# Forty-two runs of unread TensorE products behind the end of a three-block model kernel

## The chip, the cores and the metric

The kernel runs as one program on one core of a Trainium2 chip. The metric is the device time in microseconds from start to end of the program, as the median of its timed executions. Engines are named as in the profile: PE is the matrix engine (PEld its weight loads), ACT the scalar engine, DVE the vector engine, POOL and SP the other two, of which SP issues most of the DMAs.

## What is computed

The reference is a chain of transformer blocks over 256 tokens of width 1024 in float32: two layers that mix attention and a long convolution for a token stream and a context stream, then one layer of dilated attention with cross attention to a memory, and at its end a mixture of 32 experts. Only the last step, the final norm of the one output (1 x 256 x 1024), is near the change:

```python
y = tf * lax.rsqrt(jnp.mean(tf * tf, axis=-1, keepdims=True) + NORM_EPS)
return (y * g.astype(jnp.float32)).astype(t.dtype)
```

## The kernel before

Each engine has a program of its own, written out in order (`tensor_program`, `scalar_program`, `vector_program`, `pool_program`, `sync_program`); they wait for each other through counting semaphores. A name such as `pe_sums.up("spread", "output")` raises a semaphore when an instruction ends, and `at(...)` with the same name is what another engine waits for. `banks` deals out the eight PSUM banks of 128 partitions by 512 float32 columns in turn; `banks.emptied(...)` is the wait for the former user of a bank.

Activations lie with features on the partitions and tokens in the columns. A weight is cut into tiles of 128 by 128. Most dense layers run in a split form (`SPLIT`, `pe_block` at line 446, `pe_pair`): weights and activations are each split into a rounded part and a remainder, both of type float32r, and a product of a tile is three single pass products, (rounded, rounded), (rounded, remainder), (remainder, rounded), accumulated over eight tiles of the feature dimension. That makes 24 PE products for an output block, each with its own weight load of 128 columns. In the first layer the moving operand has 512 columns (256 tokens and 256 of the context), in the later layers 256. The rounding is ACT's (line 434, `ACT.Copy` from float32 to float32r, 1024 columns at a time), the remainder DVE's (line 442). A product in plain float32 is two PE instructions in the trace.

The line of PE that fills waits is `pe_idle` (line 546): float32 products of the constant tile `ones` with itself, into a bank that nobody reads, so that PE isn't idle ahead of a dense stretch:

```python
for i in range(n):
    ins = pe.eng.matmul(out[:, 0:P], ones[:, :], ones[:, :], start=True, stop=True)
```

`area` is a buffer of 14336 columns a partition, with a view `area_r` of type float32r at the same addresses; through most of the kernel it holds activations, and in the mixture of experts weights of experts.

The end of the program is one chain. The last expert's output is scattered back and added (PE line 2531, DVE line 2539), ACT squares it (line 556), PE sums the squares over the features with `ones` (line 2717), ACT takes the root (line 568), DVE the reciprocal (line 579), PE spreads it over the partitions (`pe_spread`, line 539, signal `("spread", "output")`), DVE scales by it (line 591), and SP sends the result out in four DMAs (line 2735) and waits for them. PE has nothing to do after `pe_spread`, ACT nothing after line 568.

Of the kernel before, what the change touches and what calls it, by code (L numbers as in the profile page):

```python
# [13 lines left out]
ACT = mybir.ActivationFunctionType  # L14
AX = mybir.AxisListType

P = 128
# [4 lines left out]
UF, EF = UB * P, EB * P  # L22
# [248 lines left out]
def two_blocks_kernel(nc, T):  # L271
    ctx = ExitStack()
    with ctx:
# [3 lines left out]
        def sb2(name, cols):  # L277
            at = (nc.sbuf_base + 31) // 32 * 32
            t = sb(name, cols)
            return t, nc.alloc_sbuf_tensor_at(name + "_r", [P, cols], F32R, offset=at)  # L280
# [6 lines left out]
        area, area_r = sb2("area", 14336)  # L287
# [103 lines left out]
        banks = Slots([b[:, :] for b in psum])  # L391
# [8 lines left out]
        def vv(key, i=0, n=1, rows=P):  # L400
            return vec[0:rows, VEC[key] + i:VEC[key] + i + n]
# [89 lines left out]
        def pe_open(pe, site, read_by=None, root_read_by=None):  # L491
            banks.hold(read_by or (ve_norm, ("used", site)), "sum", site)
            rsts.take(root_read_by or (pe_sums, ("spread", site)), site)
# [13 lines left out]
        def pe_added(site):  # L507
            for n in range(7):
                squares.take((ve_squares, ("added", site, max(n, 1))), site, n)
            squares.take((pe_sums, (site, 7)), site, 7)  # L510
# [24 lines left out]
        def pe_spread(pe, site, cols, give=True):  # L535
            pe.wait_ge(*landed["con"])
            pe.wait_ge(*ve_norm.at("rstd", site))
            for tb in range(cols // P):
                ins = pe.eng.matmul(banks.ap("sum", site)[:, tb * P:(tb + 1) * P],
                                    rsts.ap(site)[:, tb:tb + 1].to_broadcast([P, P]), ident, start=True, stop=True)  # L540
            ins.then_inc(*pe_sums.up("spread", site))
            if give:
                banks.give("sum", site)


        def pe_idle(pe, site, n):
            out = banks.take((pe_sums, ("idle", site)), "idle", site)
            pe.wait_ge(*banks.emptied("idle", site))
            pe.wait_ge(*gp_start.at("ones"))
            for i in range(n):  # L550
                ins = pe.eng.matmul(out[:, 0:P], ones[:, :], ones[:, :], start=True, stop=True)
            ins.then_inc(*pe_sums.up("idle", site))

        def ac_square(ac, site, n, chunk, cols):
            ac.wait_ge(*squares.emptied(site, n))
            ac.eng.activation(squares.ap(site, n)[:, 0:cols], chunk, ACT.Square).then_inc(*ac_squares.up(site, n))
# [2151 lines left out]
        def pe_output(pe):  # L2708
            pe_open(pe, "output")
            out = banks.ap("sum", "output")  # L2710
            pe.wait_ge(*banks.emptied("sum", "output"))
            for pair in range(4):
                s = squares.take((pe_sums, ("output", pair)), "output", pair)
                pe.wait_ge(*ac_squares.at("output", pair))
                for c in range(2):
                    for tb in range(2):
                        ins = pe.eng.matmul(out[:, tb:tb + 1], s[:, 256 * c + tb * P:256 * c + (tb + 1) * P], ones[:, 0:1],
                                            start=pair + c + tb == 0, stop=pair == 3 and c + tb == 2)
                ins.then_inc(*pe_sums.up("output", pair))
            pe_spread(pe, "output", N)  # L2720

        def ac_output(ac):
            for pair in range(4):
                ac.wait_ge(*ve_experts.at("added", 7, pair))
                ac_square(ac, "output", pair, X2[:, 2 * pair:2 * pair + 2, :], 512)
            ac_sqrt(ac, "output", 4, N, 1024)
# [9 lines left out]
            sp.wait_ge(s_out, 64)  # L2736


        def tensor_program(pe):
            pe_mod_group(pe, 0)  # L2740
            pe_mod_group(pe, 1)
            pe_open(pe, "mix0")
            pe_added("mix0")
            pe.wait_ge(*gp_start.at("ones"))
            pe_sum_seven(pe, "mix0", 512)
            pe_sum_last(pe, "mix0", 512)
            pe_spread(pe, "mix0", 512)
            pe_mod_group(pe, 2)
            pe_mod_group(pe, 3)
            pe_idle(pe, "mix0", 12)  # L2750
            for l in range(2):
                pe_heads(pe, l)
                pe_hyena(pe, l)
                for n, a in enumerate(attention(l)):
                    pe_attend(pe, a, convolving(l, n, pe_conv_step))
                pe_merge(pe, l)
                pe_mix_out(pe, l)
                pe_gate_up(pe, l)
                pe_down(pe, l)
            pe_keys(pe)  # L2760
            pe_mixer(pe)
            pe_mixed(pe)
            pe_memory(pe)
            pe_router_steps(pe)
            pe_moe(pe)
            pe_output(pe)

        def scalar_program(ac):
            ac.eng.dma_start(vec[:, :], T["vecs"]).then_inc(*landed["vec"])
            ac.eng.dma_start(con[:, 0:NCON0], T["con"][:, 0:NCON0]).then_inc(*landed["con"])  # L2770
            ac.wait_ge(*landed["vec"])
            for s, name in enumerate(("c", "c_ctx")):
                ac.eng.activation(tc1[:, 8 * s:8 * s + 8], vv(name, 0, 8), ACT.Sigmoid).then_inc(*ac_mod.up("silu", s))
            ac_mod_group(ac, 0)
            ac.wait_ge(*landed["x"])
            for k in range(8):
                ac_square(ac, "mix0", k, X[:, k, :], 512)
            ac_mod_group(ac, 1)
            ac_sqrt_table(ac, 5, 8)
            ac_sqrt(ac, "mix0", 8, 512, 1024)  # L2780
            ac_mod_group(ac, 2)
            ac_split(ac, where["w_in", 0, 1])
            ac_mod_group(ac, 3)
            ac_norm_mod(ac, "mix0", 0, 512)
            for l in range(2):
                if l:
                    ac_norm_mod(ac, "mix1", 1, 512)
                ac_heads(ac, l)
                ac_hyena(ac, l)
                ac.eng.activation(st[:, 41:42], epsc[:, 0:1], ACT.Exp)  # L2790
                for n, a in enumerate(attention(l)):
                    ac_attend(ac, a, convolving(l, n, ac_conv_step))
                ac_merge(ac, l)
                ac_mix_out(ac, l)
                ac_norm_mod(ac, f"ffn{l}", l, tokens(l))
                ac_gate_up(ac, l)
                ac_down(ac, l)
            ac_keys(ac)
            ac_mixer(ac)
            ac_mixed(ac)  # L2800
            ac_memory(ac)
            ac_router_steps(ac)
            ac_moe(ac)
            ac_output(ac)

        def vector_program(ve):
            ve.eng.memset(sc2[:, :, :], 0.0).then_inc(*ve_mod.up("zero"))
# [234 lines left out]
```

## Time and profile before

| | |
|---|---|
| time, median of 2 runs | 2091.78 us (2089.67 and 2093.88) |
| the profiled execution | 2084.13 us |
| its span (first to last instruction or transfer) | 2082.3 us |
| mean granted clock of PE in it | 0.967 of full speed |
| PE busy | 1890.6 us, 91% of the span |
| PE weight loads busy | 1553.5 us, 75% |
| DVE busy | 1145.1 us, 55% |
| ACT busy | 903.1 us, 43% |

The profiled execution's time is 1.8 us over its span, and 7.65 us under the median of the timed runs. Busy times are of one execution. A product's duration in the trace reaches from its start to its modelled end, and products overlap: how fast a stretch of them goes is read from the distance of their starts, or from the length of a stretch and its count.

### The profile page before, as it was taken

What the parts mean: (1) busy time and instruction counts of PE and PEld (TensorE: products, weight loads), DVE (VectorE), ACT (ScalarE), POOL (GpSimd) and SP (SyncE); (2) the same over time, 40 slices, a digit from 0 to 9 for tenths busy, and PEclk for the clock granted to TensorE, in tenths of its full rate; (3) what the DMA queues carried; (4) which work ended last, traced back from release to release, by engine and by line L of the source; (5) the groups of instructions that cost most, each with busy time, mean ns of one, the idle gap of its engine ahead of it and who ended that gap; (6) DMA issues with size and microseconds to landing.
All of it is one profiled execution on the core that took longest, in us unless ns stands there. A gap on an engine that the chain in (4) does not pass through costs nothing.

```text
span 2082.3 us, 33838 instructions
## 1 busy us (share of the span) xinstructions
PE 1890.6 (91%) x14190; PEld 1553.5 (75%) x14190; DVE 1145.1 (55%) x1878; ACT 903.1 (43%) x1532; POOL 16.9 (1%) x31
## 2 busy tenths in 40 slices
PE   7999989999999999999999999999999777667666
PEld 4877668888778888798699999997898544455343
DVE  3454766776887788557666667789665111110012
ACT  4333445665756667455454555634845000000001
POOL 0000000000000000000000000000000000000000
PEclk9999999999999999999999999999999988888898
DMA  8222014553555555224056555543247999999996
GB/s 321 83 71 81 1 71 154 180 182 111 180 175 180 192 190 174 91 91 153 1 182 203 172 183 189 178 162 112 83 151 316 420 420 420 419 418 420 420 420 249
DMA packets 91121, 428.00 MB, mean 206 GB/s; under 512 B 11089, under 2 KB 12754, under 8 KB 66002
## 3 DMA queue, kind: packets, MB, share of 16 engines
q1 hardware_dynamic: 78866, 382.51, 49.4%
q10 hardware_dynamic: 12096, 43.26, 6.2%
q8 instruction: 114, 1.87, 0.4%
q14 instruction: 45, 0.37, 0.1%
HBM read 424.68 MB, written 1.05 MB: 204 GB/s over the span
## 4 chain that ended last, share of the span: by engine, by line
PE 68%; DMA 19%; DVE 5%; ACT 4%; issue 2%; SPq 1%; ACTq 0%; POOL 0%; DVEq 0%; POOLq 0%
PE bank L463 41%; PE bank L1619 8%; DMA area<-in_w 8%; DMA ring<-in_w 4%; DMA his<-in_w 4%; DMA PPT<-in_w 3%; PE bank L1198 2%; PE bank L478 2%; PE bank L2508 2%; PE bank L2464 1%; PE bank L1171 1%; PE bank L1100 1%; PE bank L2115 1%; PE bank L937 1%; PE bank L1186 1%
## 5 line engine op out<-in xcount | busy, mean ns | idle before, releaser
L442 DVE TENSOR_TENSOR ring_r<-ring,his_r 128x1024 fp32r<-128x1024 f32 x314 | 383.2, 1222 | 223.8 <-ACT his_r L434 222.3
L463 PE MATMUL bank<-HH_r,his_r 128*128 128x256 f32 (+1 forms) x1504 | 498.3, 331 | 1.6 <-DVE ring_r L442 1.6
L463 PE MATMUL bank<-HH_r,ring_r 128*128 128x256 f32 (+1 forms) x1504 | 490.8, 326 | 0.0
L463 PE MATMUL bank<-H_r,his_r 128*128 128x256 f32 (+1 forms) x1440 | 471.6, 328 | 0.0
L434 ACT ACTIVATE his_r<-ring 128x1024 fp32r<-128x1024 f32 x314 | 330.7, 1056 | 302.8 <-PE bank L463 272.1
L463 PEld LDWEIGHTS bank<-HH_r,his_r 128*128 128x128 f32 x1504 | 283.5, 188 | 35.2 <-issue 8.6
L463 PEld LDWEIGHTS bank<-HH_r,ring_r 128*128 128x128 f32 x1504 | 283.4, 188 | 24.7
L463 PEld LDWEIGHTS bank<-H_r,his_r 128*128 128x128 f32 x1440 | 270.7, 188 | 27.2 <-issue 1.0
L2480 DVE TENSOR_TENSOR tmp<-tmp,bank 128x128 f32<-128x128 f32 x64 | 18.4, 287 | 384.3 <-ACT tmp L2473 257.2
L463 PE MATMUL bank<-area_r,his_r 128*128 128x256 f32 (+1 forms) x480 | 148.9, 323 | 0.0
L2464 PE MATMUL bank<-area,KF 128*32 128x128 f32 x1888 | 89.2, 312 | 47.5 <-DMA area<-in_w 38.9
L1619 PE MATMUL bank<-VT_r,ring_r 128*128 128x512 f32 (+1 forms) x352 | 118.6, 337 | 0.0
L2464 PEld LDWEIGHTS bank<-area,KF 128*32 128x32 f32 x1888 | 71.5, 126 | 62.8 <-DMA area<-in_w 49.5
L1619 PE MATMUL bank<-YF_r,his_r 128*128 128x512 f32 (+1 forms) x352 | 118.3, 336 | 0.0
L1619 PE MATMUL bank<-VT_r,his_r 128*128 128x512 f32 (+1 forms) x352 | 117.6, 334 | 0.0
L463 PEld LDWEIGHTS bank<-area_r,his_r 128*128 128x128 f32 x480 | 89.8, 189 | 7.6
L2519 ACT ACTIVATE H<-bank 128x512 f32<-128x512 f32 x16 | 9.6, 597 | 187.7 <-PE bank L2508 187.7
L712 ACT ACTIVATE rst<-rst 128x1024 f32<-128x1024 f32 x80 | 83.5, 1044 | 0.6 <-DVE rst L704 0.6
L2508 PE MATMUL bank<-area,tmp 128*32 128x512 f32 x256 | 55.5, 643 | 22.3 <-DMA area<-in_w 22.3
L1346 ACT ACTIVATE VT_r<-area 128x512 fp32r<-128x512 f32 (+1 forms) x96 | 49.9, 523 | 51.0 <-PE bank L1619 45.3
L1619 PEld LDWEIGHTS bank<-YF_r,his_r 128*128 128x128 f32 x352 | 66.1, 188 | 7.7
L1619 PEld LDWEIGHTS bank<-VT_r,his_r 128*128 128x128 f32 x352 | 66.2, 188 | 7.5 <-DVE YF_r L1350 0.2
(418 smaller groups left out, 3316.9 us busy)
## 6 DMA issues: line engine op xcount, KB each, us to landing
area<-in_w SPq DMA_DIRECT2D x91, 1024.0 KB, 27.3
ring<-in_w_in SPq DMA_DIRECT2D x102, 512.0 KB, 3.5
ring<-in_w_gate_up SPq DMA_DIRECT2D x88, 512.0 KB, 3.5
ring<-in_w SPq DMA_DIRECT2D x36, 1024.0 KB, 27.0
HH<-in_w SPq DMA_DIRECT2D x26, 1024.0 KB, 26.8
ring<-in_w_down SPq DMA_DIRECT2D x44, 512.0 KB, 4.3
KX<-in_w_mod_rows ACTq DMA_DIRECT2D x28, 512.0 KB, 3.4
VX<-in_w_mod_rows ACTq DMA_DIRECT2D x28, 512.0 KB, 3.5
```

The costliest lines, as they stand in the source:

```text
L434: ac.eng.activation(hi_slot(n), stream.slot(u), ACT.Copy).then_inc(*ac_hi.up(n))
L442: ve.eng.tensor_tensor(lo_slot(u), stream.slot(u), hi_slot(n).bitcast(F32), ALU.subtract).then_inc(*ve_lo.up(n))
L463: ins = pe.eng.matmul(out, a, b, start=k == 0 and m == 0, stop=end)
L478: ins = pe.eng.matmul(out, a, b, start=k + m == 0, stop=k == 7 and m == 2)
L712: ac.eng.activation(prod, prod, ACT.Copy, accum_out=MODS[l][:, j, s:s + 1]).then_inc(*ac_mod.up("sum", n, s))
L937: ins = pe.eng.matmul(vb[tb // 2][:, o:o + 256], x[:, k, sl], w, start=k == 0 and n == 0 and o == 0, stop=k == 7 and n == 2 and o > 0)
L1100: ins = pe.eng.matmul(b, cc(nm, 256 * tb + fb * P), VT[:, 2 * s + tb, :], start=tb == 0, stop=tb == 1)
L1198: ins = pe.eng.matmul(out[:, 0:256], vs(kc), c.pts[g % 2][:, kc * 256:(kc + 1) * 256], start=kc == 0, stop=kc == c.nk - 1)
L1346: ac.eng.activation(hi, src, ACT.Copy).then_inc(*ac_cut.up(*key))
L1619: ins = pe.eng.matmul(banks.ap("ff", l, 4 * half + n)[:, 0:t], w, x, start=k == 0 and i == 0, stop=k == 21 and i == 2)
L2464: ins = pe.eng.matmul(out[32 * n:32 * n + 32, 0:P], HG[g % 2][:, k, 32 * j:32 * j + 32], w, start=k == 0, stop=k == 7, tile_position=(0, 3 ...
L2508: ins = pe.eng.matmul(out[32 * j:32 * j + 32, :], AT[j][:, 32 * k:32 * k + 32], w, start=k == 0, stop=k == 3, tile_position=(0, 32 * j))
```

## The change

`tensor_program` gets `pe_bench` as its last step, and `scalar_program` a last step of 14 copies. Nothing that was there is touched: no instruction is removed or moved.

- ACT, once PE has spread the final norm, rounds the whole of `area` in place to float32r, in 14 instructions of 1024 columns. The last one signals `bench`.
- PE waits for that signal, and issues `pe_idle` with 40 products.
- Then come 21 runs with 512 columns of moving operand and 21 with 256. A run is one accumulation into a bank: 24 single pass products for 512 columns (8 tiles, 3 passes), 48 for 256 columns (twice 8 tiles, 3 passes). Behind each run stands one product of 64 columns into the same bank, with the signal of the run. That is 504 products of 512 columns, 1008 of 256 and 42 of 64.
- The first run of each width is the plain one (tiles and passes as in the kernel's split form, weights at column 0 and 1024 of `area_r`, moving operands at 4096 and 8192). The others differ from it in one thing: weights begin 8, 16, 32 or 64 columns later; moving operands 8, 16 or 32 columns later; the second moving operand lies 16 or 256 columns beyond 4096 from the first; the same weights each time, the same moving operand each time, or both; another order of the passes; all weights from column 12288 or 2048; one column repeated as the moving operand (step 0); one column repeated as the weights; weights with a step of two columns; a moving operand with a step of two columns. The last, 21st run is the plain one again, its products dealt in turn to two banks.
- No one reads the banks, and `area` is not used again.

```diff
--- before.py
+++ after.py
@@ -2736,6 +2736,41 @@
             sp.wait_ge(s_out, 64)
 
 
+        def bench_plain(n, w0=0, m0=0, low=4096, same_w=False, same_m=False, order=((0, 0), (0, 1), (1, 0)), w_at=0, m_at=4096):
+            out = []
+            for k in (list(range(8)) if n > 256 else list(range(8)) * 2):
+                for wl, ml in order:
+                    w = w_at + (0 if same_w else 1024 * wl + P * k) + w0
+                    m = m_at + (0 if same_m else low * ml + 512 * k) + m0
+                    out.append((area_r[:, w:w + P], area_r[:, m:m + n]))
+            return out
+
+        def bench_runs(n):
+            wide = [(w, area_r[:, 4096:4097].to_broadcast([P, n])) for w, _ in bench_plain(n)]
+            flat = [(area_r[:, 0:1].to_broadcast([P, P]), m) for _, m in bench_plain(n)]
+            apart = [(area_r[:, 0:2 * P:2], m) for _, m in bench_plain(n)]
+            spread = [(w, area_r[:, 4096:4096 + 2 * n:2]) for w, _ in bench_plain(n)]
+            return [bench_plain(n), bench_plain(n, w0=8), bench_plain(n, w0=16), bench_plain(n, w0=32), bench_plain(n, w0=64),
+                    bench_plain(n, m0=8), bench_plain(n, m0=16), bench_plain(n, m0=32), bench_plain(n, low=4096 + 16),
+                    bench_plain(n, low=4096 + 256), bench_plain(n, same_w=True), bench_plain(n, same_m=True),
+                    bench_plain(n, same_w=True, same_m=True), bench_plain(n, order=((0, 0), (1, 0), (0, 1))),
+                    bench_plain(n, w_at=12288), bench_plain(n, w_at=2048), wide, flat, apart, spread]
+
+        def pe_bench(pe):
+            pe.wait_ge(*ac_out.at("bench"))
+            pe_idle(pe, "bench", 40)
+            for n in (512, 256):
+                for r, run in enumerate(bench_runs(n) + [bench_runs(n)[0]]):
+                    two = [banks.take((pe_sums, ("bench", n, r)), "bench", n, r, i) for i in range(2)]
+                    for i in range(2):
+                        pe.wait_ge(*banks.emptied("bench", n, r, i))
+                    last = int(r == len(bench_runs(n)))
+                    for i, (w, m) in enumerate(run):
+                        out = two[i % 2 * last]
+                        pe.eng.matmul(out[:, 0:n], w, m, start=i <= last, stop=i >= len(run) - 1 - last)
+                    pe.eng.matmul(two[0][:, 0:64], area_r[:, 0:P], area_r[:, 0:64], start=True, stop=True).then_inc(
+                        *pe_sums.up("bench", n, r))
+
         def tensor_program(pe):
             pe_mod_group(pe, 0)
             pe_mod_group(pe, 1)
@@ -2764,6 +2799,7 @@
             pe_router_steps(pe)
             pe_moe(pe)
             pe_output(pe)
+            pe_bench(pe)
 
         def scalar_program(ac):
             ac.eng.dma_start(vec[:, :], T["vecs"]).then_inc(*landed["vec"])
@@ -2802,6 +2838,10 @@
             ac_router_steps(ac)
             ac_moe(ac)
             ac_output(ac)
+            ac.wait_ge(*pe_sums.at("spread", "output"))
+            for i in range(14):
+                ins = ac.eng.activation(area_r[:, i * UF:(i + 1) * UF], area[:, i * UF:(i + 1) * UF], ACT.Copy)
+            ins.then_inc(*ac_out.up("bench"))
 
         def vector_program(ve):
             ve.eng.memset(sc2[:, :, :], 0.0).then_inc(*ve_mod.up("zero"))
```

## Rows read from the trace of the kernel before

**Rows 1.** The page: the span, and the busy time of PE and ACT.

```profile
span 2082.3 us, 33838 instructions
PE 1890.6 (91%) x14190; PEld 1553.5 (75%) x14190; DVE 1145.1 (55%) x1878; ACT 903.1 (43%) x1532; POOL 16.9 (1%) x31
```

**Rows 2.** The chain that ended last, its end: start us, us, what.

```profile
2071.45 3.52 PE bank L2717 x32
...
2075.51 0.72 PE bank L539 x4
2076.24 0.02 issue
2076.26 0.48 DVE H L591
2076.74 0.39 DVEq L273
2077.13 2.35 DVE H L591 x6
```

**Rows 3.** Timeline of all engines from 2076: start us, us, engine and line.

```profile
2076.26 3.22 DVE L591 SCALAR_TENSOR_TENSOR H<-X,vec,bank 128x256 f32<-128x256 f32 x8 [0.80 <-PE bank L539]
2077.16 2.72 SPq L2735 DMA_DIRECT2D out<-H  x4
```

**Rows 4.** Windows at the end: PE, PEld, DVE, ACT, POOL busy, granted clock, DMA.

```profile
2070.00:2076.00 6.00, 5.45 (x43) 5.21 (x41) 1.99 (x4) 2.40 (x5) 0.00 (x0) 1.00 0.00 0
2076.00:2082.00 6.00, 0.22 (x2) 0.03 (x1) 3.22 (x8) 0.00 (x0) 0.00 (x0) 0.54 0.53 175
```

**Rows 5.** Timeline of ACT, three roundings in a row at 304.

```profile
304.60 2.93 ACT L434 ACTIVATE his_r<-ring 128x1024 fp32r<-128x1024 f32 x3
```

**Rows 6.** Groups by line and form, ACT's roundings: count, busy us, mean ns.

```profile
L434 ACT ACTIVATE his_r<-ring 128x1024 fp32r<-128x1024 f32 x314 | 330.7, 1056 | 302.8 <-PE bank L463 272.1 <-PE bank L2115 8.3 <-PE bank L937 8.2
```

**Rows 7.** Timelines of PE, two stretches of `pe_idle` with 14 products.

```profile
499.01 3.29 PE L551 MATMUL bank<-ones 128*128 128x128 f32 x28
...
885.45 4.83 PE L551 MATMUL bank<-ones 128*128 128x128 f32 x28
```

**Rows 8.** Windows over the second of these and after it, columns as above.

```profile
885.40:888.70 3.30, 3.30 (x18) 3.30 (x17) 2.23 (x4) 2.22 (x5) 0.69 (x2) 0.50 0.02 5
888.70:890.00 1.30, 1.30 (x13) 1.30 (x13) 1.30 (x3) 1.27 (x3) 0.82 (x1) 1.00 0.00 0
```

**Rows 9.** The chain, dense stretches with 512 columns.

```profile
161.93 38.49 PE bank L463 x168
...
307.58 187.20 PE bank L463 x816
...
626.42 131.84 PE bank L463 x576
```

**Rows 10.** The chain, dense stretches with 256 columns.

```profile
947.38 32.66 PE bank L463 x288
...
1153.32 65.29 PE bank L463 x576
...
1231.25 39.58 PE bank L463 x336
...
1270.83 56.80 PE bank L1619 x480
```

**Rows 11.** Windows over dense stretches of both widths, columns as above.

```profile
162.00:200.00 38.00, 38.00 (x167) 31.21 (x166) 19.08 (x22) 11.87 (x14) 0.00 (x0) 1.00 0.26 83
626.00:758.00 132.00, 132.00 (x577) 108.27 (x577) 100.13 (x98) 85.12 (x137) 0.00 (x0) 1.00 0.57 185
```

**Rows 12.** Timeline of PE where one-column products interrupt a dense stretch.

```profile
1218.32 0.28 PE L463 MATMUL bank<-HH_r,ring_r 128*128 128x256 f32 x1
1218.44 0.50 PE L516 MATMUL bank<-ones,tmp 128*128 128x1 f32 x4
1218.81 0.59 PE L523 MATMUL bank<-ones,tmp 128*128 128x1 f32 x4
1219.25 0.36 PE L463 MATMUL bank<-HH_r,his_r 128*128 128x256 f32 x1
1219.45 0.28 PE L463 MATMUL bank<-H_r,his_r 128*128 128x256 f32 x1
```

**Rows 13.** Groups by line and form, products of 512 columns from various tiles.

```profile
L463 PE MATMUL bank<-HH_r,ring_r 128*128 128x512 f32 x624 | 245.2, 393 | 0.0
...
L1619 PE MATMUL bank<-YF_r,his_r 128*128 128x512 f32 x176 | 69.0, 392 | 0.0
...
L463 PE MATMUL bank<-area_r,his_r 128*128 128x512 f32 x176 | 66.4, 392 | 0.0
```

## What it will do to the time

> **What bounds the kernel now.** I began with the page [rows 1]: PE is busy for 91% of 2082.3 us, so the body of the kernel is PE's. But the diff touches none of the body, so what counts is what the end of the span hangs on. The chain of waits, read at its end [rows 2], shows it: PE's last product, the spread of the norm (L539), ends at 2076.23, DVE scales for the remaining time, and the four output DMAs start beside it [rows 3]. The window from 2076 to 2082 shows PE and ACT with nothing to do, and a granted clock of 0.54 in the mean, so mostly the lower level of 1.2 GHz [rows 4]. The reader should see two things: between the spread and the end lie only 6.1 us, and this is all the cover that new work on ACT and PE can have. Everything in the change waits for that spread, so nothing of it can slide forward under the dense body.
>
> **The work ahead of the runs.** ACT waits for the spread. DVE began 0.02 us after it [rows 2]; ACT should begin as early, at 2076.26. It then makes 14 roundings of 1024 columns, the same instruction as L434, which takes 1056 ns by itself [rows 6]. In a row they overlap a little: three take 2.93 us [rows 5], so (2.93 - 1.06) / 2 = 0.94 us from start to start. 13 x 0.94 + 1.06 = 13.3 us, to 2089.6. That the source and target are the same columns changes nothing that the rows would show; ACT touches nothing else. The waits of this kernel's engines on each other cost 0.02 to 0.05 us, so PE starts at 2089.65.
>
> PE then issues 40 idle products, which are 80 instructions, as 14 are 28 in the trace. At the full clock 28 take 3.29 us from the first start to the last end [rows 7]; taking off the last one's 0.28 leaves 27 distances of 0.1115 us. 80 of these are 8.9 us. PE has then been idle for 13 us and sits at the lower level. The second stretch of 28 shows the price: 4.83 us instead of 3.29, and its first 3.3 us stand at a granted clock of 0.50, after which it is 1.00 [rows 7, 8]. So one such stretch at the low level costs 1.5 us; two would cost some 3.1. I take a value between, 2.4, and so 11.3 us. PE stands at 2100.9, at 2.4 GHz, when the runs begin.
>
> **The runs.** The plain runs repeat the order of the kernel's own split products, so the dense stretches are the rows to use. With 512 columns: 168 in 38.49, 816 in 187.20, 576 in 131.84 us [rows 9], which is 229.1, 229.4 and 228.9 ns each. I take 229.0: 504 x 0.229 = 115.4 us. With 256 columns there are two paces: 288 in 32.66 and 576 in 65.29 are 113.4 ns, 336 in 39.58 and 480 in 56.80 are 117.8 and 118.3 [rows 10]. The pace holds through a whole stretch and changes only after an interruption, such as the one-column products at 1218 [rows 12]: 113 ahead of them, 117.8 behind. The bench interrupts itself after every run with a product of 64 columns, and more of the long stretches stand at the slower pace, so I take 117.8: 1008 x 0.1178 = 118.7 us. All at the faster pace would be 114.3, which is 4.4 less.
>
> Is that pace right for a bench that runs alone, with no DMA and an idle DVE and ACT? A stretch with a DMA share of 0.26 and ACT busy for a third of it goes at 229.1, one with 0.57 and ACT busy for two thirds at 228.9 [rows 9, 11]. So I see no contention that could fall away. The Trainium skill, page "TensorE: Matmul & The Clock Gate", section Back-to-back issue gap, gives N / 2.4 + 2.5 ns for a single product's gap, that is 215.8 and 109.2 ns here. By that rule the runs would take 108.8 + 110.1 = 218.9 us rather than 234.1, and the total would come out 15.2 lower; the trace disagrees with it for float32r at both widths, by 13 ns at 512 columns.
>
> **Between the runs.** The 42 products of 64 columns are cheaper than a weight load: a product of one column, two instructions each, keeps a distance of about 0.1 us (eight instructions from 1218.44 to 1219.25, 0.81 us) [rows 12]. The next product's successor then came 0.20 instead of 0.118 us later [rows 12], a further 0.08. So a boundary costs 0.10 to 0.19 us; I take 0.15, and 42 x 0.15 = 6.3 us. The waits for the banks cost nothing: the bank of a run was last used by a run about three before it, or by work finished ahead of the spread, except the spread's own bank, which DVE has done with by 2079.5 [rows 3], 10 us ahead.
>
> **The odd operands.** Offsets of 8 to 64 columns, repeated tiles, other passes, other places in `area`: the rows show products from `HH_r`, `YF_r` and `area_r` with weights from two buffers, all at 392 or 393 ns of duration [rows 13], so I cost these at nothing. A gain is excluded only at 512 columns by the 213.3 ns that the columns themselves need at 2.4 GHz. No row has a moving operand or weights with a step of two or zero. From below: a step costs nothing. From above, each fetch takes twice as long: for the moving operand 24 x 0.213 + 48 x 0.107 = 10.2 us for both widths; for the weights, with 0.1115 us as the distance that a weight load allows [rows 7], 0.223 is still hidden under 0.229 at 512 columns, and at 256 costs 48 x (0.223 - 0.118) = 5.0. Together 15.2 us. I take the lower end, since the rows closest to them, all with a step of one, show the pace set by neither the tile nor its place.
>
> The Trainium skill, page "SBUF — State Buffer", section Door 1, says that two hits in a line of 16 bytes suffice for full bandwidth. By that rule a step of two float32 columns costs nothing; no run here shows it yet.
>
> **The sum.** 2076.26 + 13.3 + 0.05 + 11.3 + 115.4 + 118.7 + 6.3 = 2341.3, and 0.3 for the last product's end: a span of 2341.6 against 2082.3, 259.3 us more. With the 1.8 us around the span the profiled execution would go from 2084.1 to 2343.4. The median of the timed runs stands 7.65 us above it; I add to the median: 2091.8 + 259.3 = 2351.1 us. The output DMAs, at the end before, end 250 us early and drop off the chain.
>
> **The rivals.** First, the forecast with steps that cost (chance 0.20): one or both of the stepped fetches, or an offset or a place in `area`, halves the rate of a run. One width of a doubled run costs about 5 us, all four cases together 15.2: 2356 to 2366. For it: these are the things that no row covers. Against it: two of the forty-two runs each way are all that can be hit so.
>
> Second, the columns alone set the pace (0.06). If what adds 16 ns to each product of 512 columns is the other engines' work, it goes away behind the end: 512 / 2.4 GHz is 213.3 ns, 256 is 106.7, together 107.5 + 107.5 = 215.0 instead of 234.1, and 2332 us. Against it stands the comparison of stretches with little and much beside them [rows 9, 11]. The rule of the Trainium skill's TensorE page, told above, would put the time at 2336, close to this.
>
> Third, the clock stays low (0.03). If something in these runs, such as repeated operands, keeps PE at 1.2 GHz throughout, columns take 426.7 and 213.3 ns: 215.0 + 215.0 = 430 us, 196 more, 2547 us. Against it: the level rose within one stretch of idle products [rows 8], and it is 1.00 through every dense stretch [rows 11].
>
> Fourth, the other side: not slower (0.03). The products are read by nobody. If the build drops work without a reader, neither ACT's copies nor the runs exist, the price falls to nothing and the time is 2091.8. It would decide as soon as unread results are removed at all. Against it: the idle products have no reader either, and they stand in the trace, 28 and 28 of them [rows 7]. Hiding can't give this result, for the cover is 6.1 us and the work 265.
>
> **How the numbers follow.** The forecast as summed has 0.68. Its own range: 4.4 down for the fast pace, 2 either way for the boundaries, 1 for the idle products, and the 7.65 us between median and profiled execution, since it isn't known where the next median falls: 2340 to 2356. Reaching into the first rival gives 2338 to 2366, which holds about 0.8. A measurement of this kernel can tell a change of about 2% from none, 42 us; the forecast is 12.4% slower, and only the fourth rival is inside. Slower 0.97, same 0.03, faster 0.
>
> **What would show it.** In the profile after: the body unchanged up to 2076; a block of 14 ACT instructions of 13.3 us, PE idle under it; 80 instructions of L551 in about 11 us, of which the first 3 to 7 at 0.5 of the clock; then a PE timeline with 504 starts 0.229 apart and 1008 starts 0.113 or 0.118 apart, the granted clock at 1.00 to the end, and DMA at zero. The runs with a step of two and those with one repeated column are the last ones of each width ahead of the plain repeat, so a cost of theirs shows as longer spacing there alone. The forecast is wrong if the spacing of the plain run differs from the kernel's own, if a boundary shows a gap of half a microsecond, or if any odd run is slowed by more than a fifth.

## The result, and the profile after

The changed kernel takes 2361.87 us (median of 2 runs, 2359.17 and 2364.57) against 2091.78: a ratio of 1.129, with a 95% interval of 1.127 to 1.132. The forecast was 2351, with a range of 2338 to 2366.

The page of the kernel after, its first lines and the sum of the new products:

```profile
span 2357.4 us, 37123 instructions
PE 2154.4 (91%) x15824; PEld 1791.1 (76%) x15824; DVE 1145.8 (49%) x1878; ACT 916.8 (39%) x1546; POOL 16.9 (1%) x31
...
L2770 PE MATMUL bank<-area_r 128*128 128x256 f32 (+1 forms) x1512 | 250.4, 328 | 0.0
```

It answers to [rows 1]. PE gained 1634 instructions: 80 idle ones, 1512 products and 42 of 64 columns. ACT gained 14, DVE none.

The chain that ended last, in order of time, around the end of the old kernel and through the runs of 512 columns (L2843 are the roundings, L551 the idle products, L2770 the runs, L2771 the products of 64 columns):

```profile
2081.65 0.72 PE bank L539 x4
2082.38 0.02 issue
2082.40 2.95 ACT area_r L2843 x3
2085.35 0.95 ACTq L273
2086.30 9.47 ACT area_r L2843 x10
2095.77 0.04 issue
2095.81 11.10 PE bank L551 x80
2106.91 5.47 PE bank L2770 x24
2112.38 0.03 PE bank L2771
2112.41 5.67 PE bank L2770 x24
...
2163.36 5.55 PE bank L2770 x24
...
2196.84 5.33 PE bank L2770 x24
...
2202.20 5.64 PE bank L2770 x24
...
2207.87 5.73 PE bank L2770 x24
...
2213.63 10.93 PE bank L2770 x24
...
2224.60 5.55 PE bank L2770 x24
```

and at the end, with 256 columns:

```profile
2317.16 5.83 PE bank L2770 x48
...
2323.02 5.45 PE bank L2770 x48
...
2328.51 5.68 PE bank L2770 x48
...
2334.22 5.85 PE bank L2770 x48
...
2340.10 11.10 PE bank L2770 x48
...
2351.24 5.83 PE bank L2770 x48
```

Read it against the order of the variants. A plain run takes 5.55 us, one with the weights 8 columns later 5.67 (2112.41). The last five of each width are: one column repeated as moving operand (5.33 and 5.45), one column repeated as weights (5.64, 5.68), weights with a step of two (5.73, 5.85), the moving operand with a step of two (10.93 and 11.10), and the plain run again. So one variant of twenty is dear, and it costs 10.7 us over both widths: 10.93 - 5.55 and 11.10 - 5.83.

The end of the span moved by 275.1 us. The spread of the norm ends at 2082.37, where it ended at 2076.23 [rows 2]: 6.1 us are in the body, which the change doesn't touch. From the spread to the end it is 275.03 us instead of 6.07, so the new work is worth 269.0 us.

The 6.1 us of the body are in part a lottery that the rows of before already hinted at. The same 576 products of a dense stretch with 256 columns, in the chain after:

```profile
1158.19 68.08 PE bank L463 x576
```

They took 65.29 us in the profile before [rows 10]: 118.2 ns a product against 113.4, in the same code. Of the twelve profiles taken of kernels with this body, the changed kernel and the experiments without padding among them, two show this stretch settled at 113.3 ns and ten at 117.8, and none shows anything between. The most of the 6.1 us arose earlier: the stretch that starts at 626.42 in the profile of before [rows 9] starts at 631.04 here, and no run was made to find out why. Seven runs of the kernel before, taken beside the first experiment, spread over 2089.26 to 2101.5 us, so a body longer by 6 us is nothing unusual.

### The profile page after: what moved, and what is told of

Its sections match the earlier page's. It is cut to its first block, busy times and chain, and to the rows that moved or that the text cites. A ratio compares the mean times of both kernels' runs of the same rounds, so it can differ in the third digit from the quotient of the medians.

```text
span 2357.4 us, 37123 instructions
## 1 busy us (share of the span) xinstructions
PE 2154.4 (91%) x15824; PEld 1791.1 (76%) x15824; DVE 1145.8 (49%) x1878; ACT 916.8 (39%) x1546; POOL 16.9 (1%) x31
## 3 DMA queue, kind: packets, MB, share of 16 engines
HBM read 424.68 MB, written 1.05 MB: 181 GB/s over the span
## 4 chain that ended last, share of the span: by engine, by line
PE 68%; DMA 17%; DVE 7%; ACT 4%; issue 2%; SPq 1%; ACTq 0%; POOL 0%; POOLq 0%; DVEq 0%
PE bank L463 36%; PE bank L2770 11%; PE bank L1619 7%; DMA area<-in_w 6%; DMA ring<-in_w 4%; DMA his<-in_w 2%; DMA PPT<-in_w 2%; PE bank L2464 1%; PE bank L478 1%; PE bank L1198 1%; DMA con<-in_w 1%; DMA HH<-in_w 1%; DVE st L1270 1%; PE bank L2115 1%; PE bank L2508 1%
## 5 line engine op out<-in xcount | busy, mean ns | idle before, releaser
L463 PEld LDWEIGHTS bank<-HH_r,his_r 128*128 128x128 f32 x1504 | 282.8, 188 | 36.8 <-issue 11.6
L2770 PE MATMUL bank<-area_r 128*128 128x256 f32 (+1 forms) x1512 | 250.4, 328 | 0.0
L2770 PEld LDWEIGHTS bank<-area_r 128*128 128x128 f32 x1512 | 218.5, 191 | 25.6 <-issue 5.6
L1619 PE MATMUL bank<-VT_r,his_r 128*128 128x512 f32 (+1 forms) x352 | 118.6, 337 | 0.0
L1619 PE MATMUL bank<-YF_r,his_r 128*128 128x512 f32 (+1 forms) x352 | 117.5, 334 | 0.0
L1619 PEld LDWEIGHTS bank<-VT_r,ring_r 128*128 128x128 f32 x352 | 66.0, 187 | 7.7
```

The source lines that it names most:

```text
L463: ins = pe.eng.matmul(out, a, b, start=k == 0 and m == 0, stop=end)
L1619: ins = pe.eng.matmul(banks.ap("ff", l, 4 * half + n)[:, 0:t], w, x, start=k == 0 and i == 0, stop=k == 21 and i == 2)
L2770: pe.eng.matmul(out[:, 0:n], w, m, start=i <= last, stop=i >= len(run) - 1 - last)
```

## The experiments

In the experiments the "settled" spacing of a run is the mean of the last twelve distances between the starts of its products in the trace; its first few distances are longer while it settles.

**The stepped operand alone.** The edit:

```diff
-            spread = [(w, area_r[:, 4096:4096 + 2 * n:2]) for w, _ in bench_plain(n)]
+            spread = bench_plain(n)
```

> The moving operand with a step of two columns is replaced by the plain operands, in one run of each width. My theory (the step doubles the time of a product, the one odd operand that costs in full): these two runs fall from 11.0 and 11.1 us to 5.6 and 5.8 us, all others stay, so 10.6 to 10.7 us go, and the ratio to the kernel before falls from 1.129 to 1.124. Rival (the two runs are slow for their place in the order, or for what ran before them): they stay above 10 us and the ratio stays.

Measured: 2350.65 us (median of 4), a ratio of 1.122 with an interval of 1.118 to 1.125, which holds 1.124 and no longer holds 1.129. The run in the place of the dear one, in the chain, with its neighbours:

```profile
2211.36 5.73 PE bank L2770 x24
...
2217.12 5.54 PE bank L2770 x24
...
2222.70 5.55 PE bank L2770 x24
```

With 256 columns the run in that place took 5.86 us instead of 11.14, from its start to the next run's. From the end of the spread to the start of the last run it is 257.8 us instead of 268.7, 10.9 less. The step was the cause, and the place was not.

**What a step costs.** The twenty variants are exchanged for steps and pieces; the core of the edit:

```diff
+            def mv(step):
+                return [(w, area_r[:, 4096:4096 + step * n:step]) for w, _ in bench_plain(n)]
+            def wt(step):
+                return [(area_r[:, 0:step * P:step], m) for _, m in bench_plain(n)]
+            def part(a, b):
+                return [(w, area_r[:, 4096:4096 + n // a * b].rearrange("p (x y) -> p x y", y=b)[:, :, 0:a]) for w, _ in bench_plain(n)]
```

> The 20 variants of each width are exchanged: moving operands with a step of 1, 2, 3, 4, 8 and 0 columns; moving operands in pieces, 2 of 4 columns, 4 of 8, 8 of 16, 2 of 3, 16 of 32; weights with a step of 1, 2, 3, 4, 8 and 0; both with a step of two. Theory A (any gap between neighbouring columns breaks a paired read of two columns, so each column is read alone): every step above 1 gives 452 and 228 ns a product, and pieces of two or more adjacent columns stay near 230 and 118. Theory B (the bytes spanned count): step 3 gives about 680 ns, step 4 about 900, 2 of 4 columns as slow as a step of two, about 452. Theory C (two hits in a line of 16 bytes suffice, as the notes say): a step of 2 and 2 of 4 are alike, and a step of 4 is slower than a step of 2. Weights: in the changed kernel a step of two cost only 3% at 512 columns and nothing at 256, where a halved rate of loading would show as about 228 ns; if loading has no paired read, steps of 3, 4 and 8 cost no more either.

Settled spacings, worked out from the starts in the trace, in ns:

| moving operand | 512 columns | 256 | weights | 512 | 256 |
|---|---|---|---|---|---|
| contiguous | 226.7 | 120.0 | contiguous | 226.7 | 120.0 |
| step 2 | 453.3 | 230.0 | step 2 | 233.3 | 120.0 |
| step 3 | 450.0 | 226.7 | step 3 | 235.5 | 173.3 |
| step 4 | 461.5 | 233.3 | step 4 | 236.7 | 233.3 |
| step 8 | 431.1 | 217.8 | step 8 | 244.4 | 240.0 |
| step 0 | 218.6 | 112.0 | step 0 | 231.7 | 113.3 |
| 2 of 4 | 453.3 | 230.0 | | | |
| 2 of 3 | 340.0 | 173.3 | | | |
| 4 of 8 | 233.3 | 117.8 | both operands with step 2 | 453.3 | 233.3 |
| 8 of 16 | 233.3 | 120.8 | | | |
| 16 of 32 | 240.0 | 120.0 | | | |

Theory A fails at 2 of 4: adjacent columns, and still twice the time. Theory B fails at steps of 3, 4 and 8, which cost no more than 2. Theory C fails too: a step of two columns of float32, two hits in 16 bytes, costs the moving operand all of a doubling. For the weights it costs 7 ns at 512 columns and nothing at 256. Larger steps cost the weights 9 to 18 ns at 512 columns and 53 to 120 at 256; that the long products hide most of a slower load is my reading, and no run separates it.

**Pieces.** Sixteen shapes of pieces and steps, cut as above with a first column of choice.

> The 20 variants of each width are moving operands in pieces: 2 of 4 columns beginning at column 0, 1 and 3 of a group of four; 2 of 8; 4 of 8 beginning at 0, 1 and 2; 4 of 5; 4 of 6; 4 of 12; 8 of 12 beginning at 0 and 2; 16 of 20 beginning at 0 and 2; steps of 5, 6 and 16; plain ones beginning 1 or 2 columns later. Theory D, formed on the steps run: the moving operand is read in aligned groups of four columns; a group of which two or more are wanted takes the time of four columns, one with a single wanted column the time of two. That gives, as multiples of the time of a contiguous operand (227 to 233 ns at 512 columns): 2 for all of 2 of 4 and 2 of 8; 1 for 4 of 8 at 0 and 4 of 12; 1.5 for 4 of 8 at 1, 2 for it at 2; 1.25 for 4 of 5; 1.5 for 4 of 6; 1 and 1.5 for 8 of 12; 1 and 1.25 for 16 of 20; 2 for the steps; 1 for a shift by 1 or 2. Rival E (a gap costs by the piece, whatever its place): 4 of 8 costs the same at 0, 1 and 2, and 8 of 12 and 16 of 20 at 0 and 2.

At 512 columns, in multiples of the contiguous 226.7 ns: 2 of 4 from column 0, 1 and 3 and 2 of 8: 2.0; 4 of 8 from 0: 1.02, from 1: 2.0, from 2: 2.0; 4 of 5: 1.25; 4 of 6: 1.5; 4 of 12: 1.0; 8 of 12 from 0: 1.03, from 2: 1.5; 16 of 20 from 0: 1.06, from 2: 1.25; steps of 5, 6 and 16: 1.9 to 2.0; shifted by 1 or 2 columns: 1.05 and 1.02. Rows of the chain, 4 of 8 from column 0, 1 and 2:

```profile
2155.98 5.63 PE bank L2775 x24
2161.64 10.94 PE bank L2775 x24
2172.61 10.99 PE bank L2775 x24
```

Rival E is out: the place within a group of four columns (16 bytes) decides. Theory D is right but for 4 of 8 from column 1, where it wanted 1.5.

**A rule for groups, tried on new shapes.**

> Seventeen new shapes of moving operand and three of weights, to try a rule fitted to the two runs before. Theory G: PE fetches the moving operand in accesses of four cycles; one access brings those next wanted columns that lie in one aligned group of four, and at least the next two wherever they lie. Theory D (as in the pieces run): a group with two or more wanted columns costs four cycles, with one wanted column two. Theory T: every touched group costs four. Times over a contiguous operand (227 to 233 ns at 512 columns), G / D / T: 4 of 8 from column 3: 2 / 1.5 / 2; 4 of 7: 1.75 / 1.5 / 1.75; 4 of 9: 1.5 / 1.5 / 1.75; 2 of 5: 2 / 2 / 2.5; 2 of 6 from column 3: 2 / 2 / 3; 2 of 7: 2 / 2 / 2.5; 8 of 9: 1.125 by all; 8 of 10: 1.25 by all; 8 of 12 from 1 or from 3 and 8 of 16 from 1: 1.5 / 1.25 / 1.5; 4 of 10: 1.5 by all; 8 of 11: 1.375 / 1.25 / 1.375; 16 of 17: 1.06 by all; 2 of 5 from 3: 2 / 2 / 2.5; 4 of 6 from 2: 1.5 by all. Weights with a step of 5, 6 and 16 at 256 columns: 233 to 240 ns like steps of 4 and 8, if each touched group costs a weight load four cycles.

There were sixteen shapes of the moving operand, not seventeen. Measured (settled, at 512 columns, over 226.7): 4 of 8 from 3: 2.09; 4 of 7: 1.56; 4 of 9: 1.50; 2 of 5: 2.01; 2 of 6 from 3: 2.00; 2 of 7: 2.03; 8 of 9: 1.15; 8 of 10: 1.25; 8 of 12 from 1 and from 3: 1.50; 8 of 16 from 1: 1.44; 4 of 10: 1.54; 8 of 11: 1.28; 16 of 17: 1.07; 2 of 5 from 3: 2.03; 4 of 6 from 2: 1.53. Weights with steps of 5, 6 and 16 at 256 columns: 228.1, 228.9 and 220.0. Theory G is near in fourteen of sixteen and wrong at 4 of 7 and 8 of 11, where D is right; D is wrong at the four shapes of 4 or 8 columns that begin at 1 or 3; T is wrong at every shape of pairs that it put above 2, and at 4 of 7, 4 of 9 and 8 of 11. The weights came out 4 to 20 ns under the 233 to 240 expected. What stands: full aligned groups of four go within 6% of full pace, a cut group mostly costs as if it were whole (less at 4 of 7, 4 of 9 and 8 of 11), and nothing costs much more than twice (2.09 at most). The exact rule for cut groups stays open.

**Where the operands begin.** Plain runs whose weights begin w and moving operands m columns later:

```diff
+            pairs = ((0, 0), (8, 0), (16, 0), (24, 0), (32, 0), (40, 0), (48, 0), (56, 0), (4, 0), (0, 4), (0, 8), (0, 16), (0, 32),
+                     (0, 48), (8, 8), (16, 16), (32, 32), (16, 32), (48, 48), (32, 16))
+            return [bench_plain(n, w0=a, m0=b) for a, b in pairs]
```

> The 20 variants of each width are exchanged for plain runs whose weights begin w columns later and whose moving operands m columns later, with w and m from 0 to 56. In the changed kernel the settled spacing at 512 columns was 226 to 227 ns for the plain run and for offsets of 64 or 256, and 231 to 237 in the mean for 8, 16 and 32. Theory A (the distance of the two operands modulo 64 columns counts): (8,8), (16,16), (32,32) and (48,48) are back at 226 to 227, and (16,32) is like (0,16). Theory B (each operand's own start counts): (16,16) is slow like (16,0) or (0,16). At 256 columns the plain run had 120 to 121.5, and an offset of 16 in either operand 113 to 115; theory A then gives 121.5 for (16,16), theory B 113 to 115.

Settled spacings by the distance w - m, modulo 64 columns:

| distance | runs (w, m) | 512 columns | 256 columns |
|---|---|---|---|
| 0 | (0,0) (8,8) (16,16) (32,32) (48,48) | 226.7 in all | 120.0 in all |
| 4 | (4,0) | 226.7 | 118.7 |
| 8 | (8,0) | 233.3 | 118.6 |
| 16 | (16,0) (0,48) (32,16) | 233.3 in all | 113.3 in all |
| 24 | (24,0) | 234.6 | 117.5 |
| 32 | (32,0) (0,32) | 232.5, 232.9 | 118.2, 120.0 |
| 40 | (40,0) | 233.3 | 120.0 |
| 48 | (48,0) (0,16) (16,32) | 228.9 in all | 117.8 in all |
| 56 | (56,0) (0,8) | 233.3 in both | 116.7 in both |
| 60 | (0,4) | 231.7 | 113.3 |

Theory A holds, theory B falls at (16,16) and each other equal pair. What counts is how far apart the two reads begin, modulo 64 columns or 256 bytes, and not where either begins. With 256 columns the distance doesn't settle it alone: the run (0,16) has 117.8 ns here and had 113.3 in the changed kernel.

**Carried over to the body.** Adding up the allocations, each rounded up to 8 columns, puts the body's weights 48 columns from its activations. The edit, in the kernel before and without a bench, with 16 and with 32 columns:

```diff
+        pad = sb("pad", 16)
         ring, ringr = sb2("ring", NS * UF)
```

> The kernel before, without any bench, with an unused buffer of 16 columns ahead of the weight ring, so that ring and rounded weights begin 16 columns later and the activations stay. Theory A carried over to the body (the distance of weights and moving operand modulo 64 columns sets the pace): adding up the allocations puts the body's weights 48 columns from the moving operands, and 48 is the distance whose bench runs settle at 228.9 and at 117.8 or 113.3, as the body does. With the pad the distance is 0: the dense stretches of 512 columns go from 229.0 to 226.7 ns, those of 256 from 117.8 or 113.3 to 120.0. Rival (the body's 229.0 has other causes, such as the waits for weights or other engines): 229.0 and 117.8 stay.

> As the run before, with 32 columns: a distance of 16, whose bench runs settle at 233.3 ns at 512 columns and at 113.3 or 117.8 at 256. Theory A: dense stretches of 512 columns at 233.3, of 256 at 113.3 or 117.8. Rival: 229.0 and 117.8 stay.

The chain of the kernel with 16 columns of padding, the stretches that answer to two of [rows 9, 10]:

```profile
627.58 130.59 PE bank L464 x576
...
1157.78 69.24 PE bank L464 x576
```

and with 32 columns:

```profile
634.60 134.40 PE bank L464 x576
...
1163.46 68.08 PE bank L464 x576
...
1244.18 38.09 PE bank L464 x336
```

576 products of 512 columns took 131.84 us before; they take 130.59 (226.7 ns each) at distance 0 and 134.40 (233.3) at distance 16. With 256 columns all dense stretches of the first pad settle at 119.4 to 120.4 ns, and those of the second at about 113.3 or 117.8, in turns. An unused buffer of 64 bytes a partition moves the pace of the body's dense stretches, just as the bench says. It makes no better kernel that anything here shows: what one width gains the other loses, and the single runs, 2098.42 and 2092.95 us beside 2090.82, lie within the spread of the kernel before. A layout with distance 0 for the wide layers and 16 for the rest was not tried.

**Is it the company?** ACT and DVE work beside the runs, until some 2320 of 2363.6 us, in buffers that no run reads:

```diff
+            for i in range(230):
+                if i >= 3:
+                    ac.wait_ge(*ac_angles.at("busy", i - 3))
+                ac.eng.activation(his_flat[:, i % 3 * UF:(i % 3 + 1) * UF], hh_flat[:, 0:UF], ACT.Copy).then_inc(*ac_angles.up("busy", i))
+            for i in range(200):
+                if i >= 6:
+                    ve.wait_ge(*ve_angles.at("busy", i - 6))
+                ve.eng.tensor_tensor(ring[:, i % 6 * UF:(i % 6 + 1) * UF], hh_flat[:, UF:2 * UF], hh_flat[:, 2 * UF:3 * UF], ALU.subtract).then_inc(*ve_angles.up("busy", i))
```

> ACT makes 230 copies and DVE 200 subtractions of 1024 columns beside the runs, in buffers that no run reads, so the bench no longer runs alone. My theory (other engines' work on SBUF doesn't reach PE's reads; the kernel's own 229 ns and 117.8 ns come from where its operands lie): the runs keep their spacing within 0.5 ns, 5.58 us a plain run of 512 columns, 5.86 of 256. Rival (the second rival of the prediction turned round: what other engines do costs PE some ns a product): the plain runs of 512 columns rise from a settled 226.7 to 229 ns or more, 24 x 2.3 ns = 0.06 us or more a run, and the whole bench by 1 to 3 us.

The windows over the runs of 512 columns, first of the changed kernel, then of this one (columns as in [rows 4]):

```profile
2107.00:2230.00 123.00, 123.00 (x525) 97.45 (x524) 0.00 (x0) 0.00 (x0) 0.00 (x0) 1.00 0.00 1
```

```profile
2113.00:2237.00 124.00, 124.00 (x532) 98.41 (x531) 124.00 (x110) 124.00 (x132) 0.00 (x0) 1.00 0.00 1
```

DVE and ACT went from nothing to fully busy. From the first run's start to the last run's start it is 244.43 us against 244.41. The work of the other two engines costs PE nothing here. This run has no DMAs beside it, but the padded body has: at distance 0 its 512 column products come 226.7 ns apart with DMAs, ACT and DVE at work, like the plain run of the bench that is alone.

**The product of 64 columns.** Left out, the run's last product signals:

```diff
-                    pe.eng.matmul(two[0][:, 0:64], area_r[:, 0:P], area_r[:, 0:64], start=True, stop=True).then_inc(
-                        *pe_sums.up("bench", n, r))
+                    ins.then_inc(*pe_sums.up("bench", n, r))
```

> The 42 products of 64 columns are gone; the last product of a run signals. In the changed kernel the start of a 64 column product is followed by the next run's first product after 29 to 31 ns, and that by the second after 313 (512 columns) or 200 (256) instead of some 231 and 118. My theory (the 64 columns are too few to hide the weight load behind them, so its rest lies open once a run): without them a boundary looks like any other pair of products, the first distance of a run is about 231 and 118, and 42 x 0.11 = 4.7 us go from the bench. Rival (the opening of an accumulation in another bank or the signal costs): the first distance stays near 313 and 200, and only 42 x 0.03 = 1.2 us go.

The chain now shows one piece:

```profile
2111.09 245.85 PE bank L2770 x1512
```

The changed kernel needed 250.2 us for the same products and the 42 narrow ones (2106.91 to 2357.10): 4.3 us, 0.10 a run. The first distance of a run of 512 columns is 226 to 237 ns instead of some 313, apart from the very first run (314) and the runs of and right behind the repeated and the stepped operand, whatever bank it opens. So the cost was the narrow product's, as expected, and not that of the bank or the signal; why it costs this, my theory of the open weight load, isn't shown. The runs at distance 16 and 48 with 256 columns settled at 117.8 ns here and at 113.3 in the changed kernel.

**One run, twenty phases.** All variants are the plain run with the moving operands 16 columns later, and ahead of run r stand r products of 96 columns:

```diff
+            return [bench_plain(n, m0=16) for _ in range(20)]
...
+                    for _ in range(r):
+                        pe.eng.matmul(two[0][:, 0:96], area_r[:, 0:P], area_r[:, 0:96], start=True, stop=True)
```

> All 20 variants of a width are the same run, the moving operands 16 columns later, which at 256 columns settled at 113.3 in the changed kernel and at 117.8 in the offsets run, just as the dense stretches of the body settle at 113.3 or 117.8. Ahead of run r stand r products of 96 columns, so that the run starts at another phase. My theory (two patterns of product and weight load that each sustain themselves, chosen at the start of a stretch): within this kernel some runs of 256 columns settle at 113.3 and others at 117.8, and none between; at 512 columns all settle at 228.9. Rival (the pace is a matter of what lies where in a build): all 20 settle at the same value.

It came out the other way round. With 256 columns all settled at 117.8; with 512 columns four runs of the twenty-one (r = 5, 9, 13, 17) settled at 233.3 and the others at 228.9, where I had expected one value. In the chain, r = 4 and 5:

```profile
2135.56 5.58 PE bank L2768 x24
2141.74 5.67 PE bank L2768 x24
```

So equal products in one execution do settle at two paces, by what stands ahead of them; that it is the phase at which they begin is inferred. With 256 columns the rival's outcome came, one value. It isn't a value for this distance once and for all, as the changed kernel has 113.3. Which phases lead to which pace, and why 256 columns showed only one here, is open.

**The clock.** The 40 idle products are left out.

> The 40 idle products ahead of the runs are left out, so the runs start at a granted clock of 0.5. My theory: the low stretch of some 3.4 to 6.8 us falls on the first run, whose first 8 to 16 products come 427 ns apart instead of 227; the last run starts 11.1 us less 1.7 to 3.4 us earlier, seen from the spread of the norm, so 7.7 to 9.4 us. Rival (the third rival of the prediction): the clock stays low through the runs, and they take some 430 us instead of 250.

The windows at the start of the runs:

```profile
2091.60:2095.00 3.40, 3.38 (x8) 2.74 (x9) 0.00 (x0) 0.00 (x0) 0.00 (x0) 0.50 0.00 0
2095.00:2099.00 4.00, 4.00 (x19) 3.24 (x19) 0.00 (x0) 0.00 (x0) 0.00 (x0) 0.98 0.00 0
2099.00:2340.00 241.00, 241.00 (x1501) 215.32 (x1500) 0.00 (x0) 0.00 (x0) 0.00 (x0) 1.00 0.00 1
```

The first distances are 590 and then seven of 426 or 427 ns at 1.2 GHz (granted clock 0.50), 224 to 236 afterwards at 2.4 GHz (1.00). The last run starts 9.2 us earlier after the spread (259.5 instead of 268.7). The 10.9 us of idle products thus spared 1.7 us of slow clock. They stood behind the wait for ACT and not in it, on the chain themselves; idle products that fill a wait, as in the kernel's own use, were not tried.

**Without the runs.** The loop over the widths is empty, copies and idle products stay.

> The copies of ACT and the 40 idle products stay, the 42 runs are left out. By the prediction's sum the span ends 0.02 + 13.4 + 0.04 + 11.1 + 0.2 = 24.8 us after the spread of the norm instead of 6.1, 18.7 us more, a ratio of 1.009. Rival (that the new work slides under what is there, or that the body changes because PE and ACT have more to do): a ratio within 0.002 of 1, or a spread of the norm later by more than the 6 us that executions differ by.

Measured: 2109.23 us, a ratio of 1.008 with an interval of 1.005 to 1.010, and the chain ends 24.2 us after the spread's end at 2087.84, where the sum gave 24.8:

```profile
2087.86 2.95 ACT area_r L2843 x3
...
2101.27 10.78 PE bank L551 x80
```

Nothing of it slid under the body. The spread came 11.6 us later than in the profile of before, more than the 6 us that I had allowed. That is one of the rival's conditions. But the profiled execution was the slowest of the four timed (2114.11 us), and their median is 17.3 us over the kernel before, no more than the sum's 18, so I take the shift for the spread between executions; it isn't shown.

## Why the prediction was right

The change is slower by its own length, as all was placed behind the spread, where the only cover is 6.1 us. The sum itself was too low: 2361.87 is 10.8 us over it and outside the 2340 to 2356 that the prediction gave to it, and only the reach into the first rival holds the result. Step by step, in the profile after:

- ACT's copies: 13.3 us forecast, 13.4 measured. The start 0.02 us behind the spread, right.
- The idle products: 11.3 forecast, 10.9 to the first run's start (2095.81 to 2106.66). The clock was 0.5 for the first 4 us, which cost 1.9; I had charged 2.4, between 1.5 and 3.1.
- The runs of 512 columns with their boundaries: 118.6 forecast. They took 123.4 (2106.66 to 2230.02), of which 5.4 are the stepped run's excess, so 118.0 without it.
- The runs of 256 columns: 121.8 forecast, 127.1 measured, 121.8 without the stepped run's 5.3.

So the sum came out 9.7 us short of 269.0, and the term at fault is one: the odd operands, which I put at nothing with an upper end of 15.2. The moving operand's step of two alone cost 10.7, and the rest of the sum missed by 1.0 the other way. The bound from above for it was a fetch that takes twice as long (10.2), and the measured cost is a little over it: the whole spacing doubled, 226.7 to 453.3 ns, and not the columns' 213.3 alone. The weights' step, bound 5.0, cost 0.2 at 512 columns and nothing at 256. I had argued that the rows nearest to these cases, all with a step of one, speak for no cost. They could not: no row had a step at all, and a bound with nothing to choose inside it should have been weighed evenly. The first rival, with a chance of 0.20, described the outcome, 2356 to 2366; the forecast as summed, with 0.68, did not. Two of the prediction's own signs of being wrong came: odd runs slowed by more than a fifth (10.97 us against 5.58), and a plain run that is paced other than the kernel's own (226.7 against 229.0).

That the median is 10.8 over the forecast, close to the 9.7 of the new work, is partly luck. The body of the profile after was 6.1 us longer, and this execution stood 2.7 us under the median of the timed runs, where the one before stood 7.65 under: 9.7 + 6.1 - 4.95 = 10.8. One reading of the rows was loose: DVE's scaling ends at 2079.48 [rows 3], and the output DMAs, not DVE, make the last 2.8 us before the old end. The cover stays 6.1 us either way.

Two errors inside the run terms cancelled. With 512 columns I took 229.0 ns and 0.15 us for a boundary, 5.65 us a run; the plain one settles at 226.7 and takes 5.58 with its boundary, the runs with a shifted operand 5.60 to 5.72. The narrow product costs 0.10 us a run rather than 0.15. With 256 columns I took 117.8, 5.80 us a run; the plain run settles at 120.0 and takes 5.86, the shifted ones 5.56 to 5.87. The reason is the distance of the operands, which the body has at 48 and the plain run at 0: the body's pace was the right order of size and the wrong number. That offsets cost nothing was wrong by up to 7 ns a product, at 512 columns upwards and at 256 mostly downwards, and right in the sum, by luck: some 0.7 us more at 512 columns and 0.9 less at 256.

The second rival, company that costs PE some ns, is dead: neither its absence in the bench nor its presence in the experiment changed the pace. The third, a clock that stays low, and the fourth, work that isn't done, didn't occur: the granted clock is 1.00 from 2099.8 to the end and all 1512 products are in the trace. The rule of N / 2.4 + 2.5 ns from the Trainium skill, page "TensorE: Matmul & The Clock Gate", section Back-to-back issue gap, given there for a single product's gap, is met by no run here: contiguous operands come to 226.7 and 113.3 ns at best, one column repeated to 218.6 and 112.0, against its 215.8 and 109.2. The Trainium skill, page "SBUF — State Buffer", section Door 1, has two hits in a line of 16 bytes suffice for full bandwidth; the trace disagrees for the moving operand, as a step of two float32r columns doubles the time (453.3 ns).

## What to carry to other kernels

Work behind the last result costs its full length: find what it waits for and what still runs then, and add up the rest. When an edit brings an operand shape that no row of the trace has, price it at both ends and let the middle of the range say so; for a float32r moving operand, read whole aligned groups of four columns or pay up to about double (2.09 times at most here). And a dense stretch has its own pace in ns a product: before comparing two versions by a few tenths of a per cent, look whether a moved buffer or a changed phase has merely switched it.

## What the runs showed of the hardware that I had not expected

- The distance between the start of the weights and of the moving operand, modulo 64 float32 columns, sets the spacing of products: for starts at multiples of four columns from 226.7 to 234.6 ns at 512 columns, from 113.3 to 120.0 at 256 (one column off, 238.7 and 123.3), with the best distance for one width among the worst for the other. Sixteen columns of padding moved the body from 229.0 to 226.7 and from 117.8 or 113.3 to 120.0.
- The same products can settle at two paces, 113.3 or 117.8 ns, and 228.9 or 233.3, and keep the one they fell into, at 256 columns for hundreds of products. Between the profiles of two kernels with the same body this alone changed a stretch of 576 products by 2.8 us.
- A moving operand of one repeated column goes faster than any contiguous one, 218.6 ns at 512 columns and 112.0 at 256.
- A fetch of the moving operand with gaps costs by the cut groups of four columns, up to about twice; weights pay for a step from three columns on with 256 columns (120.0, 173.3, 233.3 ns at steps of 2, 3 and 4) and little with 512 (233.3, 235.5, 236.7).
